# Recurrent layer of a two-block network: ten output slabs multiplied as three fp32r passes instead of one f32 multiply, and an output placed six steps behind its row instead of five

## The reference, cut to what matters

```python
def odd_layer(z, w_in, conv_w, conv_b, w_a, b_a, w_x, b_x, lam, w_out):
    zp = jnp.einsum('btd,de->bte', z, w_in)
    u, gate = split_cols(zp, ODD_SPLITS)            # 2048 channels each
    ...                                             # xc: 4-tap convolution of u over time
    y = (lru_direction(xc, w_a[0], b_a[0], w_x[0], b_x[0], lam[0], reverse=False)
         + lru_direction(xc, w_a[1], b_a[1], w_x[1], b_x[1], lam[1], reverse=True))
    y = y * jax.nn.silu(gate)
    return jnp.einsum('bte,ed->btd', y, w_out)
```

## Time and profile before

| | before |
|---|---|
| median of 3 runs (lowest, highest) | 1570.5 us (1569.51, 1570.63) |
| the profiled execution's own time | 1570.01 us |
| its span, first to last instruction | 1568.2 us |
| granted TensorE clock, mean | 0.998 |
| PE busy | 1549.3 us, 99% |
| DVE busy | 1222.2 us, 78% |
| ACT busy | 891.4 us, 57% |
| POOL busy | 55.1 us, 4% |

### The profile page before, as it was taken

How to read it: one execution, slowest core, us unless ns; L and a number is a source line. 1 busy time by engine, 2 the same in 40 slices (tenths; PEclk the granted TensorE clock), 3 DMA queues, 4 the chain that set the end, 5 groups by cost and what they waited for, 6 DMA issues and landing times.

```text
span 1568.2 us, 29529 instructions
## 1 busy us (share of the span) xinstructions
PE 1549.3 (99%) x11011; PEld 1444.8 (92%) x11011; DVE 1222.2 (78%) x1888; ACT 891.4 (57%) x1404; POOL 55.1 (4%) x69
## 2 busy tenths in 40 slices
PE   8999999999999999999999999999999999999998
PEld 8888889989889999999999999999999999999997
DVE  5875677788778877798778877788778787787776
ACT  5655565587785544486646444464445865464443
POOL 0000000000001000004000000000000030000000
PEclk9999999999999999999999999999999999999999
DMA  6553224465454665545564666556564655656553
GB/s 219 151 156 99 69 81 143 167 189 173 144 160 142 204 197 181 185 152 181 150 192 157 212 189 189 184 169 203 182 197 154 189 168 148 201 172 200 179 187 121
DMA packets 74720, 264.01 MB, mean 168 GB/s; under 512 B 8528, under 2 KB 10448, under 8 KB 74640
## 3 DMA queue, kind: packets, MB, share of 16 engines
q1 hardware_dynamic: 69056, 246.76, 50.7%
q0 software_dynamic: 3824, 14.05, 2.8%
q10 hardware_dynamic: 1760, 2.09, 0.5%
HBM read 259.73 MB, written 1.05 MB: 166 GB/s over the span
## 4 chain that ended last, share of the span: by engine, by line
PE 93%; DVE 3%; ACT 2%; DMA 1%; issue 0%; ACTq 0%; SPq 0%; DVEq 0%
PE PS L1740 19%; PE PS L1732 17%; PE PS L1734 17%; PE PS L1733 16%; PE PS L1741 10%; PE PS L2016 3%; PE PS L1947 1%; PE PS L2034 1%; PE PS L2156 1%; PE PS L1937 1%; PE PS L1926 1%; PE PS L1923 1%; PE PS L1924 1%; DMA raw<-stream 1%; ACT w_hi L589 1%; DVE w_lo L1078 1%
## 5 line engine op out<-in xcount | busy, mean ns | idle before, releaser
L1078 DVE TENSOR_TENSOR w_lo<-raw,w_hi 128x1024 fp32r<-128x1024 f32 x465 | 568.8, 1233 | 90.8 <-ACT w_hi L589 85.7
L589 ACT ACTIVATE w_hi<-raw 128x1024 fp32r<-128x1024 f32 x465 | 488.3, 1053 | 85.6 <-DMA raw<-stream 41.5
L1740 PE MATMUL PS<-Y,w_hi 128*128 128x512 f32 x1280 | 450.4, 393 | 0.0
L1732 PE MATMUL PS<-Y,w_hi 128*128 128x256 f32 (+1 forms) x1468 | 429.3, 292 | 4.6 <-ACT work L787 1.8
L1734 PE MATMUL PS<-Y,w_lo 128*128 128x256 f32 (+1 forms) x1468 | 416.7, 284 | 0.0
L1733 PE MATMUL PS<-Y,w_hi 128*128 128x256 f32 (+1 forms) x1468 | 416.4, 284 | 0.0
L1741 PE MATMUL PS<-Y,w_lo 128*128 128x256 f32 x1280 | 359.1, 281 | 0.0
L1740 PEld LDWEIGHTS PS<-Y,w_hi 128*128 128x128 f32 x1280 | 240.4, 188 | 51.4
L1732 PEld LDWEIGHTS PS<-Y,w_hi 128*128 128x128 f32 x1468 | 276.8, 189 | 11.2 <-issue 6.6
L1733 PEld LDWEIGHTS PS<-Y,w_hi 128*128 128x128 f32 x1468 | 276.3, 188 | 1.9 <-issue 0.5
L1734 PEld LDWEIGHTS PS<-Y,w_lo 128*128 128x128 f32 x1468 | 276.9, 189 | 0.0
(11 more groups left out here) (331 smaller groups left out, 1627.0 us busy)
## 6 DMA issues: line engine op xcount, KB each, us to landing
raw<-stream SPq DMA_DIRECT2D x465, 512.0 KB, 4.3
work<-stream POOLq DMA_DIRECT2D x24, 512.0 KB, 4.6
work<-work ACTq DMA_DIRECT2D x10, 136.0 KB, 4.4
X<-x SPq DMA_DIRECT2D x4, 272.0 KB, 3.5
out<-zf SPq DMA_DIRECT2D x4, 256.0 KB, 2.4
work<-work ACTq DMA_DIRECT2D x20, 34.0 KB, 2.6
work<-rope SPq DMA_DIRECT2D x1, 544.0 KB, 7.6
work<-levels POOLq DMA_DIRECT2D x1, 512.0 KB, 4.0
```

What stands on the lines that cost most here:

```text
L589: act.activation(w_hi[:, s.slot, :], raw[:, s.slot % RAW, :], ACT.Copy).then_inc(hi_ready, 1)
L1078: dve.tensor_tensor(w_lo[:, s.slot, :], raw[:, s.slot % RAW, :], f32(w_hi[:, s.slot, :]), ALU.subtract).then_inc(lo_ready, 1)
L1732: pe.matmul(to, wh, xh, start=start, stop=False, skip_group_check=True)
L1740: pe.matmul(both, wh, Y[:, :, k, 0:T2], start=start, stop=False, skip_group_check=True)
```

## The change

`BEHIND` goes from 5 to 6: output k stands in step k + 6. Nine outputs (0 to 8) now stand inside the steps and seven behind step 15, where there were ten and six. Step 5 has no output any more. With `BEHIND`, the banks of the products of step 5 and the first product of step 6 change, and the order of slabs `WHOLES`.

The first ten outputs (`HALVED = 10`) are computed in three passes. ScalarE copies the slab into a high part `OH` (128x1024, fp32r) and the row into `hH` (128x256), at the end of its step k + 5, in `output_high`. GpSimd subtracts to get the low parts `OL` and `hL`, between the DMAs that it issues. TensorE waits for both low parts and issues 24 passes of 256 columns instead of 8 f32 matmuls of 256 columns. There are two buffers for each part. `output_high(k)` waits for the slab's landing, for output k - 2 on TensorE, and for the row.

```diff
-BEHIND = 5
+BEHIND = 6
+HALVED = 10
...
+        OH, OL = ([y[:, DC + 4 * b:DC + 4 * b + 4, :].rearrange("p a t -> p (a t)")[:, 0:SLAB] for b in range(2)] for y in (YH, YL))
...
                 pool.dma_start(WL[:, i % WHOLE, :], stream[E_SLABS + WHOLE_SOURCE[i]]).then_inc(whole_landed[i % WHOLE], 16)
+                kind, k = WHOLES[i - 1] if i else ("lru", 0)
+                if kind == "out" and k < HALVED:
+                    pool.wait_ge(ow_hi, k + 1)
+                    pool.tensor_tensor(OL[k % 2], WL[:, (i - 1) % WHOLE, :], f32(OH[k % 2]), ALU.subtract).then_inc(ow_lo, 1)
+                    pool.wait_ge(oy_hi, k + 1)
+                    pool.tensor_tensor(hL[:, k % 2, 0:T2], GR[:, k // 4 % 2, k % 4, :], f32(hH[:, k % 2, 0:T2]),
+                                       ALU.subtract).then_inc(oy_lo, 1)
...
+                def output_high(k):
+
+                    i = WHOLES.index(("out", k))
+                    if k >= 2:
+                        act.wait_ge(out_used, k - 1)
+                    else:
+                        act.wait_ge(w_used, ring("u", 3).n + 1)
+                    act.wait_ge(whole_landed[i % WHOLE], 16 * (i // WHOLE + 1))
+                    act.activation(OH[k % 2], WL[:, i % WHOLE, :], ACT.Copy).then_inc(ow_hi, 1)
+                    act.wait_ge(oy_ready, k + 1)
+                    act.activation(hH[:, k % 2, 0:T2], GR[:, k // 4 % 2, k % 4, :], ACT.Copy).then_inc(oy_hi, 1)
...
                         for m in inputs[1:]:
                             tap(*m)
+                        if 0 <= n + 1 - BEHIND < HALVED:
+                            output_high(n + 1 - BEHIND)
                         continue
...
                     tau(g, r)
+                    if 0 <= n + 1 - BEHIND < HALVED:
+                        output_high(n + 1 - BEHIND)
...
                     pe.wait_ge(oy_ready, n + 1)
+                    if n < HALVED:
+                        pe.wait_ge(ow_lo, n + 1)
+                        pe.wait_ge(oy_lo, n + 1)
...
-                        last = pe.matmul(PS[:, m // 2, (m % 2) * T2:(m % 2 + 1) * T2], w[:, m * P:(m + 1) * P],
-                                         GR[:, n // 4 % 2, n % 4, :], start=n == 0 and m % 2 == 0, stop=n == 15, skip_group_check=True)
+                        to, ms = PS[:, m // 2, (m % 2) * T2:(m % 2 + 1) * T2], slice(m * P, (m + 1) * P)
+                        if n < HALVED:
+                            wh, wl, yh, yl = OH[n % 2][:, ms], OL[n % 2][:, ms], hH[:, n % 2, 0:T2], hL[:, n % 2, 0:T2]
+                            pe.matmul(to, wh, yh, start=n == 0 and m % 2 == 0, stop=False, skip_group_check=True)
+                            pe.matmul(to, wh, yl, start=False, stop=False, skip_group_check=True)
+                            last = pe.matmul(to, wl, yh, start=False, stop=False, skip_group_check=True)
+                        else:
+                            last = pe.matmul(to, w[:, ms], GR[:, n // 4 % 2, n % 4, :], start=False, stop=n == 15, skip_group_check=True)
```

More of the change, by code:

```diff
@@ L345, in program @@
         tap_done, xc_ready, lru_done, lru_out = sem("tap_done"), sem("xc_ready"), sem("lru_done"), sem("lru_out")
+        ow_hi, ow_lo, oy_hi, oy_lo = sem("ow_hi"), sem("ow_lo"), sem("oy_hi"), sem("oy_lo")
         gs_ready, gp_ready, li_ready, la_ready, tau_ready, sw_ready = sem("gs_ready"), sem("gp_ready"), sem("li_ready"), sem("la_ready"), sem("tau_ready"), sem("sw_ready")
```

## The result

The changed kernel takes **1582.45 us** (median of 4 runs, 1582.13 to 1583.16), beside 1570.2 for the kernel before on the same chip: a ratio of 1.008, 95% interval [1.0068, 1.0092], or 12.3 us slower. The profiled execution has a span of 1580.0 us at a mean granted clock of 0.995 (before: 1568.2 at 0.998).

A forecast was written before the change was run, and what follows sets the result against it. TensorE, busy 99%, was taken to bound the kernel. VectorE, held up by GpSimd, would start `gates(15)` 3.8 us later and the end add 2.25: +6.0 on 1570.01, forecast 1576 us, range 1567.5 to 1581.

The forecast's parts named there:

- The passes' saving: Recurrent layer's outputs on TensorE: three passes take 2.80 us instead of 3.45, saving 0.65 each, 6.5 for ten.
- TensorE's own way to `gates(15)`, 452.6: TensorE from `gates(5)`: 443.3 without waits plus 9.3 of waits gives 452.6, 3.2 us before the old start, 455.80.
- The end, +2.25: From the start of `gates(15)` to the next layer: 28.3 us instead of 26.03, as output 9 moves there.
- The holds, 22 us: GpSimd's subtractions in the recurrent layer hold VectorE 1.7 (wide) and 0.5 us (narrow) per output, 22 for ten.
- The second rival: Only VectorE's plain TENSOR_TENSOR is held up, 10.3 of the 22 us; TensorE decides: 0, 1570.5 us; chance 0.20.
- the port is free: Rival: GpSimd's subtractions don't hold VectorE up in the layer; -0.95, about 1569.5 us; chance 0.08.
- Some idle time stays, and some holds fall into idle time ...; both are a few us and I let them cancel: VectorE up to `gated(14)`: remaining idle time and holds that cost nothing cancel, so it ends at 459.5.
- the 72.0: VectorE's own work from `gated(5)` to `gated(14)`: 72.0 us of 90.25, counting the small gaps between its instructions.
- The prediction's own sign of being wrong: VectorE still idle several us from step 10 on: then TensorE's own way decides and time falls to 1570 or below.
- Sum: Whole kernel: `gates(15)` starts 3.8 us later, the end adds 2.25, together +6.0, giving 1576 us.
- The fast rival: Neither port nor ScalarE's lateness reaches TensorE: `gates(15)` starts at 446.8; -6.75, 1564 us; chance 0.10.

The follow-up runs named there:

- Experiment 2: The change with GpSimd filling zeros (memsets, no SBUF reads) instead of subtracting, so the low parts are zero; 1568.59 us, ratio 0.9994 to the kernel before.
- experiment 10: The change, ten three-pass outputs, with the scans spread: one row per step from 4 to 14, five behind step 15; 1578.55 us, ratio 1.0052.
- experiment 5: The kernel before plus ten wide and ten narrow GpSimd subtractions into unused space, which no engine's calculation waits for; 1579.52 us, ratio 1.0067.
- experiment 3: The change without low parts: GpSimd subtracts nothing, the three passes read the high parts, outputs wait only for ScalarE's copies; 1569.28 us, ratio 0.9998.
- experiment 4: The change without ScalarE's copies and GpSimd's subtractions: the passes read whatever stands in the buffers; 1565.41 us, ratio 0.9974.
- experiment 6: The change with the ten pairs of subtractions made by VectorE at the end of its steps, not by GpSimd; 1579.57 us, ratio 1.0066.

## Why the prediction was wrong

The direction and the main mechanism were right: GpSimd's reads hold VectorE, and VectorE then sets the start of `gates(15)`. But 1576 was 6 us too low, and 1582.45 lies outside the range. By its own steps:

- **The passes' saving**: right. In the changed kernel output 0 takes 2.83 us (374.18 to 377.01) at full clock, for the forecast's 2.80. The Trainium skill, "FP8 and Floating Point Precision", section "TensorE Precision Notes", counts four passes for a true f32 product. The estimate of 4/3 in time that the prediction drew from it isn't borne out: 3.45 to 2.83 is 1.22.
- **TensorE's own way to `gates(15)`, 452.6**: right in sum, in part by luck. Experiment 2, which has no holds, starts it at 451.95, 97.0 us behind its `gates(5)` (354.99), where the forecast had 95.8. But its waits come to 6.6 us and not 9.3 (in step 6 it is 0.4, not 2.0), and a stretch at half clock, which the forecast didn't have, made up for part of it.
- **The end, +2.25**: right where the clock is full. It forecast 28.3 us behind `gates(15)`; experiment 10 has 28.4 and experiment 2 has 28.15 (480.10 - 451.95). In the change it is 29.7, since `gates(15)` ran at half clock: 4.49 us instead of 2.95, **1.5 us that the forecast didn't have**.
- **The holds, 22 us**: right in sum, 21.9 in the window. The size of a hold agrees too (1.7 and 0.4 at output 3, beside 1.7 and 0.5). The costs of the two kinds, 3.4 and 10.5 us, are no measure of the holds themselves, but divide in about the same way. GpSimd's own instructions took longer than forecast, 2.58 and 1.25 us on average beside 1.9 to 2.5 and 0.6. Where the forecast had no row, whether scans and `weighed` are held, they are: 665 to 1144 ns and 723 to 1219. The second rival, only plain TENSOR_TENSOR, is out. So is "the port is free" by experiments 2 and 5.
- **"Some idle time stays, and some holds fall into idle time ...; both are a few us and I let them cancel"**: this is the step that failed. There was next to nothing on the other side to cancel against. All twenty subtractions in the window met a busy VectorE; one narrow one ended under L1633 (at 380.61) and one in part under L1645 (at 436.11). A held instruction counts as busy, and the busy time grew by 21.9 us for the forecast's 22. So the idle time had to be added in full: 5.1 us of waits stayed, and 2.3 of small gaps (99.14 less 91.79), where the 72.0 held 2.1 of gaps. 72.0 + 22.0 + 5.1 is 99.1, the window's length. `gates(15)` came 8.9 later by it, not 3.8: **5.1 us**. The prediction's own sign of being wrong, several us of idle time from step 10 on, did come (1.5 and 2.4 us in steps 12 and 13). It was tied to the wrong outcome: the idle time made VectorE's way longer, and did not leave the decision to TensorE.
- **Sum**: 3.8 + 5.1 is 8.9, 2.25 + 1.5 is 3.75, together 12.6 for the layer's 12.5 and the medians' 12.3.
- **The fast rival** named its point well: it wanted under 10 us of holds and idle together. It failed by the holds, but not by them alone: experiment 3 has none and still starts `gates(15)` at 451.45, not 446.8. Experiments 3 and 4 add that even then little was to be had: passes alone save 4.1, and ScalarE's copies take 3.9 back.

What the 5.1 us of waits are: three waits of before, at the same places. The one for the convolution's input shrank from 2.6 to 1.2 us, the one for the roots of step 12 from 2.1 to 1.5, and the one for the slab of step 13 grew from 2.1 to 2.4. The last stands like this in the timelines of VectorE of the kernel before, of experiment 3 and of the change:

```profile
446.63 1.23 DVE L1078 TENSOR_TENSOR w_lo<-raw,w_hi 128x1024 fp32r<-128x1024 f32 x1 [2.08 <-ACT w_hi L589]
442.28 1.23 DVE L1104 TENSOR_TENSOR w_lo<-raw,w_hi 128x1024 fp32r<-128x1024 f32 x1 [2.39 <-ACT w_hi L599]
450.05 1.23 DVE L1104 TENSOR_TENSOR w_lo<-raw,w_hi 128x1024 fp32r<-128x1024 f32 x1 [2.39 <-ACT w_hi L599]
```

Experiment 3 has no stretch at half clock in this layer and the same 2.39 us, so this wait isn't the clock's work. ScalarE's list puts decays ahead of that slab's high part, before and after. All three could be read in the kernel before.

No run takes the clock drops away while it leaves the holds, so how the 12.3 us divide between holds and clock stays open, but for the 1.5 us of `gates(15)`. Two runs bear on it. In experiment 2 such a stretch stands at 430 us, behind 6 us in which TensorE was busy 3.55, and the kernel is no slower than the one before. At `gates(15)` TensorE even waits 0.21 us for VectorE:

```profile
424.00:430.00 6.00, 3.55 (x21) 2.57 (x20) 3.11 (x6) 3.91 (x8) 2.86 (x5) 1.00 0.35 130
430.00:434.00 4.00, 4.00 (x22) 4.00 (x23) 1.68 (x3) 3.97 (x4) 0.23 (x1) 0.57 0.56 161
```

And experiment 10 still has such stretches at 383, 437 and 457 us, but `gates(15)` takes its 2.85 us at full clock, and the kernel gains 3.9.

## What to carry to other kernels

Before work is moved to GpSimd, count its reads of SBUF against VectorE's: ten pairs of subtractions held VectorE for 22 us in the change and cost 9.9 us by themselves in experiment 5, while 28 us of fillings cost nothing. In a ledger of an engine that sets the end, add its holds and the waits that will stay. Read those waits one by one, by place, from the trace of before, and don't cancel them against the holds. And look at the engine that is second before you pay for a saving on the first: here 6.5 us of TensorE's work were worth 4.1 at best, because VectorE stood right behind.

## What the runs showed of the hardware

- A GpSimd subtraction of two SBUF inputs and VectorE's TENSOR_TENSOR_SCAN or SCALAR_TENSOR_TENSOR on two SBUF inputs stop each other as two plain TENSOR_TENSOR do (L1104: 1223 to 1533 ns). The Trainium skill, "SBUF — State Buffer", section "Who interferes with whom", says it of any VectorE instruction with two SBUF inputs, and this trace bears it out (scan 665 to 1144 ns). Instructions with one input in PSUM aren't held (L1645 takes its 0.42 us at 436.46, inside a subtraction that lasts from 436.11 to 437.02), and fillings on GpSimd hold nobody (experiment 2).
- In a kernel that is 98% busy on TensorE, waits of 1.8 us and more were followed by stretches at 1.2 GHz (windows at 0.51 and 0.57). But the length of the wait alone doesn't decide it: one of 2.36 us in the change (up to 383.26) and one of 3.08 us in experiment 6 (up to 420.01) were not, while one of 2.34 us in experiment 10 (up to 381.73) was (0.57 from 382 to 386 us). An f32 output of 3.45 us took 4.86 in one of them (experiment 5, 459.49 to 464.35), 1.4 us more. A late VectorE can thus be paid twice when TensorE waits for it.
